# Moving the activation buffers of a weight-streaming kernel down by 64 bytes in each SBUF partition

## The reference

```python
memn = rmsnorm(mem, mem_norm)
for l in range(2):
    h = rmsnorm(x, mix_norm[l])
    x = x + (ab_mixer(h, ...) if l == 0 else c_mixer(h, ...))      # h @ w_in, recurrences, ... @ w_out
    x = x + mem_cross_attn(rmsnorm(x, xa_norm[l]), memn, wq, wk, wv, wo)
    x = x + square(relu(rmsnorm(x, mlp_norm[l]) @ w1)) @ w2          # 1024 -> 4096 -> 1024
x = rmsnorm(x, final_norm)
for layer in range(2):
    h = rmsnorm_2(x, attn_norm[layer])
    x = x + (fox_and_dsa(h) if layer == 0 else moba(h))             # attention, with h @ w_in and ... @ w_out
    x = x + conv_glu_ffn(rmsnorm_2(x, ffn_norm[layer]), ...)         # 1024 -> 2 x 2816 -> 1024
return rmsnorm_2(x, final_norm_2)
```

## Time and profile before

| | before |
|---|---|
| median of 3 runs | 1635.77 us (1633.54 to 1635.9) |
| the profiled execution | 1636.0 us |
| its span, first to last instruction | 1634.2 us |
| mean granted TensorE clock | 0.979 of full speed |
| matmuls, weight loads | 12,614 each |
| PE, PEld busy | 1561.1 us (96%), 1491.0 us (91%) |
| POOL, ACT, DVE busy | 1192.3, 830.4, 759.9 us |
| read from HBM | 245.11 MB, 151 GB/s over the span |

### The profile page before, as it was taken

One profiled execution on the slowest core, in us unless ns is written; L12 is line 12 of the kernel. 1 busy time (PEld: TensorE's weight loads), 2 busy tenths in 40 slices (PEclk: granted clock), 3 DMA queues, 4 the chain that ended last, 5 costly groups with the idle time before them and its releaser, 6 DMA issues. The chain is left out here.

```text
span 1634.2 us, 32576 instructions
## 1 busy us (share of the span) xinstructions
PE 1561.1 (96%) x12614; PEld 1491.0 (91%) x12614; DVE 759.9 (46%) x1385; ACT 830.4 (51%) x1250; POOL 1192.3 (73%) x920
## 2 busy tenths in 40 slices
PE   7989999999999798999999999889999999999997
PEld 6978989999998688998999998779999997899997
DVE  5554644220187656534422016945554128465522
ACT  4663555554465553555555445355545443554542
POOL 5655967999977500596799896706999987189995
PEclk9999999999999998999999999979999999899999
DMA  6433535555554200353555553405656553155663
GB/s 264 143 103 104 193 117 168 194 194 194 191 166 148 90 1 1 115 194 105 178 195 194 193 182 130 142 1 171 195 194 194 194 189 129 40 180 193 194 195 104
DMA packets 67662, 248.04 MB, mean 152 GB/s; under 512 B 7632, under 2 KB 7888, under 8 KB 67152
## 3 DMA queue, kind: packets, MB, share of 16 engines
q1 hardware_dynamic: 67536, 246.19, 45.4%
HBM read 245.11 MB, written 1.05 MB: 151 GB/s over the span
## 5 line engine op out<-in xcount | busy, mean ns | idle before, releaser
L345 POOL TENSOR_TENSOR ring_lo<-ring,ring_hi 128x512 fp32r<-128x512 f32 x916 | 1192.1, 1341 | 424.1 <-ACT ring_hi L999 421.9
L999 ACT ACTIVATE ring_hi<-ring 128x1024 fp32r<-128x1024 f32 x458 | 465.9, 1052 | 202.0 <-DMA ring<-panels 193.6
L379 PE MATMUL ps_dve<-x_hi,ring_hi 128*128 128x256 f32 x1928 | 461.0, 280 | 17.8 <-POOL ring_lo L345 11.1
L379 PE MATMUL ps_dve<-x_lo,ring_hi 128*128 128x256 f32 x1928 | 456.4, 278 | 0.0
L379 PEld LDWEIGHTS ps_dve<-x_hi,ring_hi 128*128 128x128 f32 x1928 | 364.1, 189 | 24.1 <-issue 15.6
L379 PEld LDWEIGHTS ps_dve<-x_lo,ring_hi 128*128 128x128 f32 x1928 | 364.1, 189 | 0.5 <-issue 0.2
L379 PE MATMUL ps_dve<-x_hi,ring_lo 128*128 128x256 f32 x1928 | 271.4, 278 | 0.1
L379 PEld LDWEIGHTS ps_dve<-x_hi,ring_lo 128*128 128x128 f32 x1928 | 243.6, 188 | 0.9 <-POOL ring_lo L345 0.7
L379 PE MATMUL ps_dve<-work_parts,ring_hi 128*128 128x256 f32 x1728 | 225.3, 276 | 0.0
L379 PEld LDWEIGHTS ps_dve<-work_parts,ring_hi 128*128 128x128 f32 x1728 | 211.7, 188 | 0.0
L1488 DVE TENSOR_TENSOR xT<-xT,ps_dve 128x512 f32<-128x512 f32 x40 | 27.5, 688 | 312.3 <-PE ps_dve L379 312.1
(11 more groups left out here) (285 smaller groups left out, 1997.6 us busy)
## 6 DMA issues: line engine op xcount, KB each, us to landing
ring<-panels SPq DMA_DIRECT2D x458, 512.0 KB, 3.5
consts<-constants SPq DMA_DIRECT2D x1, 1700.0 KB, 11.7
xT<-x_t SPq DMA_DIRECT2D x1, 1024.0 KB, 5.3
scratch<-mem_t SPq DMA_DIRECT2D x1, 1024.0 KB, 17.7
out_t<-xT SPq DMA_DIRECT2D x4, 256.0 KB, 2.2
smalls<-small_operands SPq DMA_DIRECT2D x1, 824.5 KB, 14.5
consts<-constants SPq DMA_DIRECT2D x1, 129.5 KB, 5.2
angle_i<-positions SPq DMA_DIRECT2D x1, 128.0 KB, 8.1
```

The costliest lines, as they stand in the source:

```text
L345: pool.tensor_tensor(ring_lo[:, s, cs], ring[:, s, cs], plain(ring_hi[:, s, cs]), ALU.subtract).then_inc(sem("lo_made"), 1)
L379: ins = pe.matmul(o, lhsT, rhs, start=start, stop=stop, skip_group_check=True)
L999: tell(act.activation(ring_hi[:, n % RING, :], ring[:, n % RING, :], ACT.Copy), "hi_made")
```

## The change

The margin ahead of `xT` is cut from 88 floats to 72.

```diff
         consts = sb("consts", [P, N_CONST])
         smalls = sb("smalls", [P, N_SMALL])
-        sb("stream_margin", [P, 88])
+        sb("stream_margin", [P, 72])
         xT = sb("xT", [P, C, T])
```

## The result

The changed kernel takes 1673.71 us (median of 4 runs, 1669.93 to 1679.32); the kernel before takes 1634.65 us (median of 4, 1633.22 to 1635.9). The ratio is 1.0236, 95% interval 1.0193 to 1.0278: about 39 us slower. The prediction said 1635.8 us with a range of 1625 to 1661. The profiled execution took 1679.32 us, with a span of 1677.5 us; counts of instructions (12,614 matmuls) and bytes (248.04 MB) are those of before.

A forecast was written before the change was run, and what follows sets the result against it. The prediction took TensorE to bound the kernel, by matmul count times pitch. Profiled execution 1636.0, less 0.2 to the median of the runs, plus 0 for the change, gave 1635.8 us; range 1625 to 1661.

The forecast's parts named there:

- What bounds the kernel, and where the change acts: TensorE sets the time, as matmul count times start-to-start pitch; any effect of the change must show in that pitch.
- Both levels stay, for both signs show both: Ring matmuls: pitches stay 113.3 and 117.6 ns, since operands 64 bytes below and 64 above each show both; 0 us.
- the term for the levels: Ring matmuls: the two pitch levels, 113.3 and 117.6 ns, don't change with the new distance; 0 us.
- The case called likeliest: Ring matmuls: the two pitches are dealt about as now, about 2,000 at the long one; 0 +/- 3 us, chance 0.25.
- The price from above: Every ring matmul at the long pitch: 8,900 x 4.3 ns = 38 us.
- everything at the long pitch: All ring matmuls at 117.6 ns: 1636 + 38 = 1674 us; chance 0.05, counted within Rival 2.
- Rival 2: Five stretches behind norm sums go to the long pitch: 6.2 us per long stretch, 26 all, 1642 to 1662; chance 0.31.
- dealt about as now, 0 +/- 3 us: Ring matmuls: about 2,000, give or take 700, stay at the long pitch, so the time changes by 0 +/- 3 us.
- Rival 3: Ring matmuls: position doesn't make the two pitches, so nothing happens at all; 1636 us, chance 0.12.
- Rivals 1 and 4: Ring matmuls: 1, long pitch vanishes, 1627 us, chance 0.26; 4, short pitch shrinks further, 1591 us at most, chance 0.06.

The follow-up runs named there:

- e3: Margin cut to 72 as in the changed kernel, plus a pad of 16 floats ahead of work, which puts work back at 64 below; 1660.55 us.
- e13: The kernel before, unchanged, profiled a second time; 1639.53 us.
- e12: The kernel of e2 once more, timed in rounds against the kernel before; ratio 1.0015 (0.9978 to 1.0052).
- e15: Margin of 24 floats where the kernel before has 88 (activations 320 bytes below the ring), timed against the kernel before; ratio 0.9995 (0.9961 to 1.003).
- e1: Kernel before with a pad of 16 floats ahead of the ring and the margin at 72: activations stay, the ring moves up 64 bytes; 1669.14 us.
- e2: Kernel before with a pad of 16 floats ahead of the ring, margin kept at 88: everything 64 bytes higher, distance unchanged; 1628.08 us.
- e5: Margin of 120 floats where the kernel before has 88 (activations 64 bytes above the ring), run once; 1648.22 us.
- e16: Margin of 120 floats (64 above, as in e5), timed in rounds against the kernel before; ratio 1.0162 (1.0107 to 1.0217).

## Why the prediction was wrong

*What bounds the kernel, and where the change acts: right.* The pitch of TensorE's ring matmuls carries all of the loss, 51.0 us against 43.3 between the profiled executions; POOL, ACT, DVE and the transfers followed or had room. e3 shows it inside one execution, buffer by buffer.

*"Both levels stay, for both signs show both": the step that failed.* I had two signs of one distance, 64 below and 64 above, both of them multiples of 64 that are not multiples of 128, and took it that no other distance would have other levels. That was no evidence about 128, and the range's upper end was built on it: at most the 117.6 ns of the trace, and that in four long stretches. The measured levels at 128 are 118.6 and 120.0 ns, so 5.3 to 6.7 ns for a matmul that was tight in place of 4.3, and every stretch has them, not the unlucky ones. So the term for the levels, put at 0, was worth 51 us. The case called likeliest had a chance of 0.25, below those of rivals 1 and 2, and could not happen.

*The price from above, 38 us and 1674 us: the right size by luck.* The measured 1673.71 lies at "everything at the long pitch" only because levels that are 1 to 2.4 ns above that pitch (51 us by the counts, against the 38 of the case) came with less time elsewhere. I gave that case 0.05 and left it outside the range. A mechanism whose direction isn't known from the trace deserved a range up to its full price.

*Rival 2 (long stretches lost behind the norm sums): its mechanism exists, in the kernel before.* e13 lost two of the five, 1,436 and 1,418 matmuls, at 4.4 ns each, 12.6 us. It is no effect of the change. So the term "dealt about as now, 0 +/- 3 us" was mis-sized too: the kernel before spreads over 1633 to 1656 us in the thirteen runs beside e12, and over 1628.92 to 1645.41 in twelve of the thirteen beside e15 (the other took 1655.39), where three runs had suggested 2.4 us. The draw is part of that spread and the granted clock, 0.979 to 0.992 in these runs, another.

*Rival 3, nothing at all: out.* The Trainium skill ("TensorE: Matmul & The Clock Gate", "Step-by-step: what each phase is for") has the two read ports of TensorE independent, and by that the distance should cost nothing. The measurement decides against it: the same instructions at the same clock go from 113.3 to 118.6 or 120.0 ns when nothing but the distance of the two operands changes (e1 against the earlier trace rows). Whether the ports or something behind them does it, no run tells.

*Rivals 1 and 4: no run showed them.* No distance that I tried has a level below 113.3 ns, and none was left with 113.3 ns alone: e2 has all its long stretches there but not its shorter bursts.

What is shown is that the relative position of stationary and moving operand, modulo 256 bytes as far as tried, sets the levels. That their reads meet in a common part of SBUF is still only the likeliest reading: it fits that the sum of both positions doesn't matter, but no run looked at a read. What picks one of two levels at the start of a stretch is open. Nor is it shown that it is picked anew in each execution of one program on one chip: e2 and e12 were profiled on different chips, e5 and e16 too, and for the first profiles of the kernels before and after the chip isn't on record. That stages alike in their code get different levels inside one profile speaks for it, as do the 16 us over which one kernel's times spread on one chip.

## What to carry to other kernels

Where a kernel streams one buffer as weights against another as moving operand, their addresses' distance modulo 256 bytes can be a tuning parameter; here it was worth up to 6% of the matmul pitch; try it in steps of 64 bytes, and pin it with a margin so that an edit to a small buffer ahead doesn't change it. Read the pitch from counts in gapless windows, not from mean durations. When two executions differ, subtract their starts one by one before the difference is put down to the change. And profile a kernel twice before a range is built on how its stretches happened to fall.

## What the runs showed of the hardware that I had not expected

- One form of matmul (fp32r, 128 x 128 weights, 256 moving columns) at a granted clock of 1.00 has pitches of 113.3, 116.7, 117.3, 117.7, 118.3, 118.6 and 120.0 ns. Which of them can occur goes with the distance of its operands; the difference between 113.3 and 118.7 ns stands with every other engine and the DMA idle.
- A stretch of 1,400 matmuls and more keeps the level that it settles on within its first few matmuls, as long as the operand pair stays the same; which of the levels that is differs between profiles of one program (113.3 in one profile of the kernel before and 117.7 in the next, in the same stretch), and is worth about 6 us a stretch.
- Both signs of 64 bytes have the same levels, but not the same time: 64 above is 1.6% slower than 64 below (e16), and in the profiles the longer level comes up more often (13 of 15 long stretches at 192 modulo 256, 6 of 25 at 64).
